# Routing of experts by tile, the first gather matrix ahead of the rounds' loop, and layer norm sums within that loop

## What is computed

```python
logits = (x @ router_w) + router_b                   # 8 experts
top_val, top_idx = lax.top_k(logits, 2)
weights = jax.nn.softmax(top_val, axis=-1)
combine = jnp.sum(one_hot(top_idx, 8) * weights[..., None], axis=-2)
for e in range(8):
    y = y + combine[..., e:e + 1] * swiglu(x, w1[e], w3[e], w2[e])   # 1024 -> 1408 -> 1024
x = layer_norm(ALPHA * x + y, ln_g, ln_b)
```

## Time and profile before

| | us |
|---|---|
| median of 3 runs | 2228.22 |
| lowest and highest of them | 2228.03, 2229.43 |
| the profiled execution | 2229.54 |
| its span | 2227.8 |
| TensorE matmuls busy in it | 2095.4 (94%) |
| VectorE busy | 884.1 (40%) |
| ScalarE busy | 374.3 (17%) |

### The profile page before, as it was taken

One profiled execution on the slowest core, in us unless ns is written; L12 is line 12 of the kernel. 1 busy time (PEld: TensorE's weight loads), 2 busy tenths in 40 slices (PEclk: granted clock), 3 DMA queues, 4 the chain that ended last, 5 costly groups with the idle time before them and its releaser, 6 DMA issues.

```text
span 2227.8 us, 37306 instructions
## 1 busy us (share of the span) xinstructions
PE 2095.4 (94%) x16128; PEld 1552.6 (70%) x16128; DVE 884.1 (40%) x1887; ACT 374.3 (17%) x891; POOL 86.6 (4%) x180
## 2 busy tenths in 40 slices
PE   8998999998999989997999999899999988999998
PEld 7786776877777877765653554387687667858886
DVE  1415425677725144242110000235568753454433
ACT  1312230000013122301010000133300012331000
POOL 3000000010000000020000000000001020000000
PEclk9999899999999998997999999999999999999999
DMA  8333234498563342426999999852568763332552
GB/s 254 103 104 126 78 140 151 169 303 284 189 174 104 98 142 77 142 79 221 348 315 376 346 334 348 291 170 93 182 220 288 255 201 115 102 114 95 170 170 95
DMA packets 333831, 421.43 MB, mean 189 GB/s; under 512 B 27222, under 2 KB 282148, under 8 KB 333668
## 3 DMA queue, kind: packets, MB, share of 16 engines
q1 hardware_dynamic: 312464, 352.96, 49.0%
q0 software_dynamic: 13408, 50.66, 6.8%
q10 hardware_dynamic: 7796, 15.43, 2.0%
HBM read 417.90 MB, written 1.05 MB: 188 GB/s over the span
## 4 chain that ended last, share of the span: by engine, by line
PE 79%; DMA 9%; DVE 6%; ACT 3%; issue 1%; ACTq 1%; SPq 0%; DVEq 0%; POOL 0%
PE psum L1266 15%; PE psum L1298 11%; PE psum L1402 10%; PE psum L1273 9%; PE psum L1283 6%; PE psum L1462 5%; DMA ring<-in_ffn_w 3%; PE psum L1919 3%; DMA ring<-in_w_up 3%; PE psum L1532 2%; PE psum L1703 2%; PE psum L1310 2%; PE psum L1730 1%; DMA arena<-in_w_mod 1%; PE psum L1391 1%
## 5 line engine op out<-in xcount | busy, mean ns | idle before, releaser
L1266 PE MATMUL psum<-xT,ring 128*128 128x256 f32 x1600 | 369.3, 391 | 3.9 <-ACT small L775 2.1
L1266 PEld LDWEIGHTS psum<-xT,ring 128*128 128x128 f32 x1600 | 309.4, 196 | 58.6 <-issue 7.5
L1283 PE MATMUL psum<-ring,arena 128*128 128x512 f32 x528 | 232.6, 593 | 2.2 <-DVE arena L2157 2.2
L1273 PE MATMUL psum<-ring,xT 128*128 128x256 f32 (+2 forms) x960 | 206.1, 374 | 11.8 <-DVE arena L2383 4.4
L1273 PEld LDWEIGHTS psum<-ring,xT 128*128 128x128 f32 x960 | 174.8, 194 | 40.3 <-DVE arena L2383 5.7
L1283 PEld LDWEIGHTS psum<-ring,arena 128*128 128x128 f32 x528 | 97.7, 190 | 114.7 <-issue 113.8
L2091 DVE SCALAR_TENSOR_TENSOR arena<-arena,cond 128x256 f32<-128x256 f32 x336 | 137.4, 479 | 0.6
L1298 PEld LDWEIGHTS psum<-xT,ring 128*128 128x128 f32 x960 | 115.8, 198 | 24.3 <-issue 24.3
L1402 PE MATMUL psum<-ring,arena 128*32 128x256 f32 x2304 | 126.9, 379 | 0.7 <-DVE arena L2227 0.7
L1298 PE MATMUL psum<-xT,ring 128*128 128x128 f32 x960 | 116.5, 281 | 10.8 <-DMA ring<-in_w_up 5.4
L1298 PE MATMUL psum<-oT,arena 128*128 128x128 f32 x960 | 119.1, 278 | 7.0 <-DVE arena L2107 6.9
(11 more groups left out here) (415 smaller groups left out, 2510.4 us busy)
## 6 DMA issues: line engine op xcount, KB each, us to landing
ring<-in_w_in SPq DMA_DIRECT2D x80, 1024.0 KB, 5.3
ring<-in_exp_w SPq DMA_DIRECT2D x312, 256.0 KB, 5.9
arena<-in_w_mod POOLq DMA_DIRECT2D x48, 1024.0 KB, 10.2
ring<-in_ffn_w SPq DMA_DIRECT2D x33, 1024.0 KB, 7.6
arena<-in_exp_w SPq DMA_DIRECT2D x120, 256.0 KB, 7.1
ring<-in_w_gate SPq DMA_DIRECT2D x22, 1024.0 KB, 8.8
ring<-in_w_up SPq DMA_DIRECT2D x22, 1024.0 KB, 11.2
ring<-in_w_down SPq DMA_DIRECT2D x22, 1024.0 KB, 5.0
```

Of the source, the lines that this page charges most:

```text
L1266: ins = pe.matmul(dst, w[:, k * 256 + c0:k * 256 + c0 + m], act_t[:, k, :], start=(k == 0), stop=(k == KT - 1))
L1273: ins = pe.matmul(dst, act_t[:, k, t * P:t * P + P], w[:, k * 256 + c0:k * 256 + c0 + n], start=(k == 0), stop=(k == KT - 1))
L1283: ins = pe.matmul(psum[:, 4 + 2 * t + h, :], gT[:, s % 2, f * 256 + t * P:f * 256 + t * P + P], w2[:, f * D + h * 512:f * D + h * 512 + 51 ...
```

## The change

Ahead of the loop: each router tile has a bank of its own and is handled when it is there; the gap goes behind `assigned`, the weights behind the gather matrices; ranks and rounds are worked out with three instructions fewer; the gather matrix of set 0 is made ahead of the loop, with two instructions a tile, and at a turn's end the one for the next turn. TensorE waits for each tile of it. In the loop: ScalarE copies the rows for the scatter in three pieces and TensorE waits for each; VectorE takes `bn_stats` of each half of a tile as soon as it has been added. Behind the loop: `bn_aggr` of both tiles first; the second pass over tile 1 goes behind the modulation of tile 0. SP waits for the router's second tile, as before.

```diff
@@ ScalarE, keep_rows_of
-                    xstep(act.copy(yb[:, d], psum[:, 3 * d:3 * d + 3, :]), "y", q, d)
+                    for r in range(3):
+                        xstep(act.copy(yb[:, d, r, :], psum[:, 3 * d + r, :]), "y", q, d, r)
@@ TensorE, gather_tokens
-                    if k == 0:
-                        pe.wait_ge(*ready("x_dve", "gather", q))
-                    free_bank(6 + k % 2, ("x_act", "x_dve")[k % 2], "xg", q, k, after="x_dve" if k == 0 else None)
+                    free_bank(6 + k % 2, ("x_act", "x_dve")[k % 2], "xg", q, k, after="x_dve" if k == 0 and q else None)
                     for t in range(NT):
+                        if k == 0:
+                            pe.wait_ge(*(ready("x_dve", "gather", q, t) if q else ready("x_pick", "next", t, back=1)))
                         ins = pe.matmul(psum[:, 6 + k % 2, 0:WIDE], x[:, t, k * P:k * P + P], gather[:, t, :],
                                         start=(t == 0), stop=(t == NT - 1))
@@ TensorE, scatter_rows
-                    if t == 0:
-                        pe.wait_ge(*ready("x_act", "y", q, d))
-                    free_bank(6 + t, "x_dve", "acc", q, d, t, after="x_act")
+                    free_bank(6 + t, "x_dve", "acc", q, d, t)
                     for r in range(3):
+                        if t == 0:
+                            pe.wait_ge(*ready("x_act", "y", q, d, r))
@@ TensorE, the router
-                            ins = pe.matmul(psum[:, 4, t * 8:t * 8 + 8], xT[:, k, t * P:t * P + P], router[:, k, :],
+                            ins = pe.matmul(psum[:, 4 + t, 0:N_EXP], xT[:, k, t * P:t * P + P], router[:, k, :],
                                             start=(k == 0), stop=(k == KT - 1))
-                    job(ins, "router")
-                    pe.wait_ge(*ready("dve", "router_logits"))
+                        job(ins, "router", t)
+                    pe.wait_ge(*ready("dve", "router_logits", NT - 1))
@@ VectorE, experts()
                 step(dve.tensor_tensor(assigned[:], onehot[:, :, 0, :], onehot[:, :, 1, :], ALU.add), "assigned")
+                step(dve.tensor_tensor(e2, top8[:, :, 1], top8[:, :, 0], ALU.subtract), "router_gap")
                 dve.wait_ge(*ready("pe_job", "ranks"))
-                for c in range(2):
-                    step(dve.tensor_tensor(ranked[:, :, c, :], onehot[:, :, c, :],
-                                           psum[:, 5, 0:16].rearrange("p (t e) -> p t e", t=NT), ALU.mult))
                 step(dve.tensor_reduce(most[:, 0:1], psum[:, 5, 16:24], AX, ALU.max))
                 step(dve.tensor_scalar(rounds[:, 0:1], most[:, 0:1], float(ROOM), 1.0, ALU.is_gt, ALU.add))
-                step(dve.tensor_scalar(rounds[:, 1:2], most[:, 0:1], float(2 * ROOM), None, ALU.is_gt))
-                step(dve.tensor_tensor(rounds[:, 0:1], rounds[:, 0:1], rounds[:, 1:2], ALU.add))
+                step(dve.scalar_tensor_tensor(out=rounds[:, 0:1], in0=most[:, 0:1], scalar=float(2 * ROOM),
+                                              in1=rounds[:, 0:1], op0=ALU.is_gt, op1=ALU.add))
                 step(dve.tensor_copy(rounds_i[:], rounds[:]), "rounds")
 
+                step(dve.tensor_tensor(ranked[:], onehot[:], psum[:, 5, 0:16].rearrange("p (t e) -> p t e", t=NT)
+                                       .unsqueeze(2).broadcast_to([P, NT, 2, N_EXP]), ALU.mult))
                 step(dve.tensor_reduce(rank[:], ranked[:], AX, ALU.add))
                 step(dve.tensor_scalar(over[:], rank[:], float(ROOM), None, ALU.is_ge))
-                step(dve.tensor_scalar(code[:], rank[:], float(2 * ROOM), None, ALU.is_ge))
-                step(dve.tensor_tensor(over[:], over[:], code[:], ALU.add))
+                step(dve.scalar_tensor_tensor(out=over[:], in0=rank[:], scalar=float(2 * ROOM), in1=over[:],
+                                              op0=ALU.is_ge, op1=ALU.add))
...
+                def pick(t, done):
+
+                    done(dve.tensor_scalar(other[:], number[:], code[:, t, 1:2], None, ALU.is_equal))
+                    return dve.scalar_tensor_tensor(out=gather[:, t, :], in0=number[:], scalar=code[:, t, 0:1],
+                                                    in1=other[:], op0=ALU.is_equal, op1=ALU.add)
+
+                for t in range(NT):
+                    pick(t, step).then_inc(*made("x_pick", "first", t))
+                    dve.wait_ge(*ready("x_pick", "first", t))
+                dve.wait_ge(*ready("act", "router_exp"))
+                step(dve.tensor_scalar(wts[:, :, 0], e2, 1.0, None, ALU.add))
+                step(dve.reciprocal(wts[:, :, 0], wts[:, :, 0]))
+                step(dve.tensor_tensor(wts[:, :, 1], wts[:, :, 0], e2, ALU.mult))
                 n_rounds = dve.value_load(rounds_i[0:1, 0:1], min_val=1, max_val=3)
...
+                def half_sums(d, t):
+
+                    step_stat = dve.bn_stats(stat[:, t, d, :], acc[:, t, d * 512:d * 512 + 512])
+                    step_stat.then_inc(*made("x_dve", "stat", d, t))
+
                 with S.turns(dve, n_rounds):
-                    pick_tokens(0)
                     keep_tokens(0)
...
+                        else:
+                            pick_tokens(SETS)
                         add_rows(q, 0)
-                    add_rows(SETS - 1, 1)
-                    dve.wait_ge(*ready("x_dve", "acc", SETS - 1, 1, 1))
+                    for d in range(2):
+                        for t in range(NT):
+                            if d == 1:
+                                add_rows(SETS - 1, 1, (t,))
+                            dve.wait_ge(*ready("x_dve", "acc", SETS - 1, d, t))
+                            half_sums(d, t)
+                    dve.wait_ge(*ready("x_dve", "stat", 1, NT - 1))
@@ VectorE, layer 1 ahead of experts()
                     for t in range(NT):
                         step(dve.tensor_scalar(acc[:, t, :], x[:, t, :], ALPHA, None, ALU.mult))
-                    dve.wait_ge(*ready("pe_job", "router"))
...
-                    for t in range(NT):
+                        dve.wait_ge(*ready("pe_job", "router", t))
+                        step(dve.tensor_tensor(logit[:, t, :], psum[:, 4 + t, 0:N_EXP], router_b[:], ALU.add),
+                             "router_logits", t)
                         step(dve.max(top8[:, t, :], logit[:, t, :]))
                         step(dve.max_index(idx8[:, t, :].bitcast(U32), top8[:, t, :], logit[:, t, :]))
                     step(dve.tensor_copy(idxf[:], idx8.bitcast(U32)))
-
-                    step(dve.tensor_tensor(e2, top8[:, :, 1], top8[:, :, 0], ALU.subtract), "router_gap")
-                    dve.wait_ge(*ready("act", "router_exp"))
-                    step(dve.tensor_scalar(wts[:, :, 0], e2, 1.0, None, ALU.add))
-                    step(dve.reciprocal(wts[:, :, 0], wts[:, :, 0]))
-                    step(dve.tensor_tensor(wts[:, :, 1], wts[:, :, 0], e2, ALU.mult))
@@ VectorE, second block, layer 0
+                    for t in range(NT):
+                        norm_sum(t, "ln2", 1)
                     dve.wait_ge(*ready("rows", "ln2", 1))
-                    norm_sums(acc, 0, "ln2", 1)
                     norm_rows(acc, 0, "ln2", 1)
-                    norm_sums(acc, 1, "ln2", 1)
                     scaled("mix", l, 0)
-                    norm_rows(acc, 1, "ln2", 1)
+                    centred(acc, 1, "ln2", 1)
...
                 modulate("mix", l, 0)
-                if l == 1:
+                if l == 0:
+                    norm_scaled(1, "ln2", 1)
+                else:
                     add_dense("ffn2", 0, 1)
```

More of the change, by code:

```diff
@@ L487, in _ @@
                     sp.wait_ge(*ready("dve", "rounds"))
-                    sp.wait_ge(*ready("pe_job", "router"))
+                    sp.wait_ge(*ready("pe_job", "router", NT - 1))
                     n_rounds = sp.value_load(rounds_i[0:1, 0:1], min_val=1, max_val=3)
@@ L2059, in norm_sums, with norm_sum, centred @@
                 dve.wait_ge(S.sem("dve"), S.count["dve"])
+                norm_sum(t, *key)
+            def norm_sum(t, *key):
                 step(dve.bn_aggr(mv[:, t, :], stat[:, t, :, :].rearrange("p h s -> p (h s)")), "var", *key, t)
             def norm_rows(src, t, *key):
+                centred(src, t, *key)
+                norm_scaled(t, *key)
+            def centred(src, t, *key):
                 dve.wait_ge(*ready("act", "sd", *key, t))
@@ L2067, in norm_rows, with norm_scaled @@
                                               in1=rows[:, 0, :], op0=ALU.subtract, op1=ALU.mult))
+            def norm_scaled(t, *key):
                 step(dve.scalar_tensor_tensor(out=x[:, t, :], in0=x[:, t, :], scalar=rs[:, t:t + 1],
@@ L2201, in experts @@
                                               op0=ALU.mult, op1=ALU.add))
+                def pick(t, done):
[9 more added lines that the diff above has]
+                step(dve.tensor_tensor(wts[:, :, 1], wts[:, :, 0], e2, ALU.mult))
```

(26 more changed lines are left out.)

## The result

The kernel after ran at 2216.61 us (median of 10 runs, 2210.2 to 2222.5) beside 2228.14 for the kernel before (10 runs, 2223.1 to 2230.9): the ratio is 0.9948, 95% interval 0.9933 to 0.9962. The forecast had been 2221.0, with a range down to 2218.0. The gain was clear, and 11.5 us and not 7.2. Two more sets of 8 runs gave 2218.45 (ratio 0.9958, 0.9942 to 0.9973) and 2219.65 (0.9962, 0.9943 to 0.9981).

What follows compares the result with a forecast made beforehand. TensorE was taken to bound the kernel, with loads next. Savings of 5.2 us ahead of the loop and 2.0 behind it make 7.2, taking the median from 2228.22 to 2221.0 us; range 2218.0 to 2224.2.

Steps and rivals of the forecast that it cites:

- Early matrix: Ahead of the loop: first gather matrix made before loop entry, two instructions a tile, waited for by tile; 3.0 us saved.
- the rest: Ahead of the loop: logits by tile 0.48, expert weights moved 1.11, fewer steps behind the ranks 0.58 us saved.
- The merged instruction: In the gather matrix: one `scalar_tensor_tensor` of 384 columns replaces compare and add; taken as 0.57 us, bounds 0.42 and 0.98.
- the second tile's wait: At the gather: tile 1's matrix follows 1.05 us later, covered at half clock; at full clock it would cost 0.4 us.
- Rival E: At the gather: TensorE meets the second wait or its own reading of the rounds; gain 4 us, 2224.2; 3%.
- SP was earlier: Ahead of the loop: SP's queue, which issues the expert loads, comes 2.2 us earlier, less than the matmuls' 5.2.
- rival D: In the loop: 14 added TensorE waits hold the array; at 0.9 us each they cost 12.6, time 2233.6; 2%.
- rival A: In the experts' loop: loads become the bound and 3.0 us of the gain go; 2224.0; 7%.
- Rival C: Behind the loop: the spread or the projection's first load limits; tail gains about 0.5, not 2.0 us; 2222.5; 7%.
- a wholly slow spread: Behind the loop: spread of the gate rows entirely at low clock lasts 6.9 us instead of 5.35; 1.5 lost.
- rival B: Clock takes another course behind the loop or at the gather: gain 9, 2219.2 (12%), or 5.5, 2222.7 (12%).
- The line of 0.2%: Whole kernel: 4.5 us, about what a measurement can tell from no change; line at 2223.8, 0.88 for faster.

Runs made afterwards that it cites:

- t_order: Kernel before with only the second pass of tile 1's layer norm moved behind the modulation of tile 0: 2226.3 us, ratio 0.9990.
- b_warm_proj: Kernel before with four added matmuls of constants in TensorE's wait ahead of the projection only: 2223.8 us, ratio 0.9991.
- the control: Kernel before, unchanged, run again against itself: 2227.5 us, ratio 0.9996.
- b_warm: Kernel before with added matmuls of constants, five ahead of the spread and four ahead of the projection: 2222.1 us, ratio 0.9978.
- e_front: Kernel before with only the edits ahead of the loop, nothing in the tail: 2219.6 us, ratio 0.9962.
- a_gap: Kernel after with the second pass of tile 1's norm put back ahead of the modulation of tile 0: 2215.8 us, ratio 0.9963.
- a_warm: Kernel after with added matmuls of constants in TensorE's waits ahead of the loop: 2216.3 us, ratio 0.9940 against the kernel before.
- all_warm: Kernel after with added matmuls of constants in all five waits, ahead of and behind the loop: 2214.9 us, ratio 0.9952 against the kernel before.

## Why the prediction was right and wrong

**Ahead of the loop: right.** 5.2 us forecast, 5.15 measured. Early matrix 3.0 (2.99), the rest 2.17 (2.16). The merged instruction costs 0.62 and not 0.57. The trace of the kernel before could have told: it has the same operation over 256 columns at 0.48 us and over 1024 at 1.285, and a line between them gives 0.61 for 384. TensorE did not meet the second tile's wait, nor its own reading of the rounds: the gather is one unbroken row of 12.79 us. Rival E did not come about. SP was earlier by 2.2, as forecast.

**In the loop: right.** 387.92 us with 14 more waits, beside 387.91, so rival D is out. (The 389.5 that the prediction calls the loop proper is its window, 1.6 us longer than the loop.) No wait of an expert matmul for a load, with DMA at 1.04 of its share: rival A is out too.

**Behind the loop: right in its sum.** 2.0 forecast, 1.97 measured; spread and diagonal end level (1421.73, 1421.69) as had been seen. Rival C did not come about. The prediction's price for a wholly slow spread, 6.9 us, was too low: the four spreads of the new tail without a fall took 3.67, which at half the rate is 7.3. No trace had one above 5.37.

**The clock: the step that failed.** The prediction put this term at nothing. It said: "For the forecast I leave both stretches as they are, moved with their work." The one behind the loop did not stay: the projection's slow stretch, worth 1.72 us, went in all nine traces with any part of the new tail. This was named, as part of rival B, at 12%, and should have been in the sum: 7.2 + 1.7 = 8.9, or 2219.3. Rival B had also tied it to a clock that is high throughout, and that was not needed: in all three traces of the kernel after the spread still fell, and the tile was fast. The evidence was in the rows, since both falls stood by gaps that the edits were to shorten; what could not be read there was whether 0.5 us less would be enough, and in t_order it was. The Trainium skill, TensorE: Matmul & The Clock Gate, What's actually happening, states that activity releases the throttle; b_warm_proj agrees, where added matmuls took the tile from 8.70 to 7.01 us. At the gather, where the forecast also took no gain, there was none.

**The scatter: under-rated.** The three sets of the kernel after have a mean of 2217.5 over 26 runs, and the 129 runs of the kernel before, in all five sets with the control, 2226.7: 9.2 us, with a standard error of 0.9. The steps and the projection's clock make 8.85. The interval of the first set (0.9933 to 0.9962) holds 8.85 us (0.9960) and not 7.2 (0.9968), so what remains of its 11.5 is within the scatter of ten runs. That the first median lay below the range, and below 2219.3 too, was luck of the draw: the two later sets gave 2218.45 and 2219.65. The scatter goes with the clock as well: slow stretches stand at places that nobody touched (at 57, 320 and 936 us, say, in some traces and not in others), and the mean granted clock of single runs, 0.969 to 0.978 in the two kernels, goes with their times (correlation -0.94 over the 107 later runs of the kernel before). The line of 0.2% for what can be told from no change was right in size; the range was too narrow on the fast side, since it was built from three runs within 1.4 us.

## What to carry to other kernels

Where TensorE waits between short pieces of work, cost the clock with the steps: list each fall in the trace, the idle time ahead of it, and which edits change that idle time. Compare edited stretches from matmul to matmul over several traces, as they repeat to hundredths of a microsecond when the whole scatters by three to four. A wait that nothing can shorten can be filled with matmuls of constants: here the next piece of work started no more than 0.05 us later for it. Whether the whole gains has to be measured, as it was clear in b_warm and not in b_warm_proj.

## What was not expected of the hardware

Work that computes nothing made the kernel before faster in its place: four matmuls of 256 columns took 1.7 us off the tile behind them (8.70 to 7.01). An idle gap of one length can be followed by a fall of the clock or not: with 1.98 us ahead of the spread it fell in three traces of seven. And a gather that was short by an early rise did not make the whole shorter in e_front, a_gap and t_order: it took 12.8 to 13.0 us, but the clock fell later in the loop, which took 389.6 instead of 387.9. That fall stands behind an idle gap of 1.99 us, some 88 us into the loop, in which TensorE waits for ScalarE. In e_front, TensorE alone and then a window behind the gap:

```profile
1113.96 0.87 PE L1448 MATMUL psum<-ident,arena 128*128 128x128 f32 x6 [1.99 <-ACT arena L712]
```

```profile
1115.00:1119.00 4.00, 4.00 (x48) 2.08 (x44) 0.00 (x0) 0.73 (x2) 0.00 (x0) 0.57 1.10 349
```

All 16 traces have this gap, at 1.99 us, and only these three have the fall behind it. In a_warm and all_warm the gather was shorter still (11.8 us) and the loop kept its 387.92, so that the early rise brings the later fall is not shown.
